# A two-block transformer kernel on one core: router on un-normalised rows, joint square roots, the last three experts written out, and out-projection weights scaled between couples of heads

## What is computed

```
h = rmsnorm(x, g_attn_norm); proj = h @ w_in            # 928 columns
mix = [rmsnorm(pool_mixer(u)), rmsnorm(mla_attention(...))]
x = x + mix @ w_out
h = rmsnorm(x, g_ffn_norm)
x = x + moe(h, w_router, ...)                           # 32 experts, top 4
x = rmsnorm(x, g_final)
# second block, modulated by mod = silu(c) @ w_ada + b_ada
hn = rms(x, norm1_g) * (1 + sc1) + sh1
y = mixer(hn, w_in_2, ...)                              # 16 heads of 3 kinds
x = x + g1 * (y @ w_out_2)
hn = rms(x, norm2_g) * (1 + sc2) + sh2
x = x + g2 * ((silu(gate) * up) @ w_down)               # gate, up = hn @ w_gate_up
```

## Time and profile before

| | |
|---|---|
| median of 3 runs | 1468.03 us (1467.84 to 1472.79) |
| profiled execution: its own time, its span | 1465.46 us, 1463.6 us |
| PE busy | 1409.3 us (96%) |
| PE weight loads | 753.7 us (51%) |
| DVE, ACT, POOL busy | 410.1, 225.0, 21.9 us |
| loaded | 497.05 MB, 340 GB/s on average |
| chain that ended last | PE 74%, DMA 21%, DVE 2%, ACT 1% |

### The profile page before, as it was taken

The page is one execution under the profiler, slowest core; times in us unless marked ns, Lnnn a source line. Parts: engine busy times, 40 slices in busy tenths (PEclk is TensorE's granted clock), DMA queues, the critical chain, the costliest instruction groups (busy, mean ns, idle before and its releaser), DMA issues.

```text
span 1463.6 us, 17945 instructions
## 1 busy us (share of the span) xinstructions
PE 1409.3 (96%) x7194; PEld 753.7 (51%) x7194; DVE 410.1 (28%) x1021; ACT 225.0 (15%) x425; POOL 21.9 (1%) x14
## 2 busy tenths in 40 slices
PE   6998999999999999999999999999899998999999
PEld 5654444444444444344334433443388864888843
DVE  5546311211211111121112111211325563001784
ACT  1332111111111111011101110111123442100000
POOL 3200000000000000000000000000000000000000
PEclk9999999999999999999999999999999999999999
DMA  9978999999999999999999999999994326444400
GB/s 340 354 294 345 413 428 428 428 429 429 428 429 428 429 429 429 428 428 429 429 429 428 428 429 429 429 428 429 415 362 169 115 87 201 141 147 145 160 12 29
DMA packets 83777, 497.05 MB, mean 340 GB/s; under 512 B 6285, under 2 KB 47962, under 8 KB 56762
## 3 DMA queue, kind: packets, MB, share of 16 engines
q1 hardware_dynamic: 83132, 495.46, 83.4%
q10 hardware_dynamic: 606, 1.06, 0.2%
HBM read 495.44 MB, written 1.05 MB: 339 GB/s over the span
## 4 chain that ended last, share of the span: by engine, by line
PE 74%; DMA 21%; DVE 2%; ACT 1%; issue 1%; SPq 0%; DVEq 0%; ACTq 0%
PE PS L955 19%; DMA ring<-in_w_gate_up_dram 13%; PE PS L981 11%; PE PS L1329 11%; DMA qk<-in_w_gate_up_dram 8%; PE PS L940 6%; PE PS L1084 6%; PE PS L1339 5%; PE PS L989 3%; PE PS L773 2%; PE PS L670 2%; PE PS L1208 2%; PE PS L967 1%; PE PS L949 1%; PE PS L962 1%
## 5 line engine op out<-in xcount | busy, mean ns | idle before, releaser
L955 PE MATMUL PS<-ring,store 128*64 128x512 f32 x1360 | 301.0, 594 | 14.0 <-DMA ring<-in_w_gate_up_dram 13.7
L955 PEld LDWEIGHTS PS<-ring,store 128*64 128x64 f32 x1360 | 94.4, 137 | 207.9 <-issue 170.7
L2073 DVE TENSOR_SCALAR store<-PS 128x512 f32<-128x512 f32 x32 | 22.1, 691 | 619.7 <-PE PS L955 619.7
L1329 PE MATMUL PS<-xc,ring 128*128 128x256 f32 x704 | 155.3, 384 | 2.3 <-DVE xc L1769 2.3
L981 PE MATMUL PS<-ring,store 128*64 128x512 f32 x704 | 154.8, 592 | 0.0
L1329 PEld LDWEIGHTS PS<-xc,ring 128*128 128x128 f32 x704 | 135.8, 193 | 21.9 <-DVE xc L1769 2.5
L940 PE MATMUL PS<-store,rows 128*128 128x64 f32 x1056 | 125.2, 272 | 1.3 <-DVE store L2051 1.3
L940 PEld LDWEIGHTS PS<-store,rows 128*128 128x128 f32 x1056 | 123.4, 192 | 2.1 <-issue 2.1
L981 PEld LDWEIGHTS PS<-ring,store 128*64 128x64 f32 x704 | 49.3, 137 | 90.7 <-issue 89.1
L1084 PE MATMUL PS<-ring,xc 128*128 128x240 f32 (+1 forms) x448 | 93.6, 366 | 0.0
L1499 ACT ACTIVATE store<-store 128x512 f32<-128x512 f32 x32 | 20.1, 629 | 452.5 <-DVE store L2073 452.5
(11 more groups left out here) (367 smaller groups left out, 1219.3 us busy)
## 6 DMA issues: line engine op xcount, KB each, us to landing
ring<-in_w_gate_up_dram SPq DMA_DIRECT2D x85, 2048.0 KB, 35.0
ring<-in_w_down_dram SPq DMA_DIRECT2D x44, 2048.0 KB, 37.3
qk<-in_w_gate_up_dram SPq DMA_DIRECT2D x21, 2048.0 KB, 37.5
ring<-in_w_ada_dram SPq DMA_DIRECT2D x24, 1024.0 KB, 15.3
store<-in_w_gate_up_dram SPq DMA_DIRECT2D x11, 2048.0 KB, 34.9
ring<-in_w_gate_up_dram SPq DMA_DIRECT2D x22, 1024.0 KB, 5.1
xc<-in_w_down_dram SPq DMA_DIRECT2D x10, 2048.0 KB, 36.5
store<-in_w_down_dram SPq DMA_DIRECT2D x10, 2048.0 KB, 37.8
```

The costliest lines, as they stand in the source:

```text
L955: mm = pe.matmul(bank(b)[CAP * h:CAP * (h + 1), :], xg[:, k, :], w[:, b * FE + h * 512:b * FE + (h + 1) * 512], start=False, stop=(k == KD ...
L1329: mm = pe.matmul(bank(4 + 2 * (j % 2) + up)[:, f * T:(f + 1) * T], chunk(n)[:, k, f * P:(f + 1) * P], cols[:, k, :], start=(k == 0), stop= ...
```

## The change

The diff touches eight places.

1. **Loads before the experts.** `ada` chunks 8 to 11 (4 MB) move behind the experts; `N_MOE` is four chunks lower. SP's order of the experts' first loads changes, `third[2]` is now at the low end of `store`, and the scratch tiles of the experts are at its high end. The bias of `ada` is loaded once and not 32 times.
2. **Columns one by one.** `need_col(k)` replaces `need_cols`; the products that follow take k in the order 0, 4, 1, 5, 2, 6, 3, 7.
3. **Sums of squares in the mixer.** VectorE adds four columns of squares (`reduce_squares`), and TensorE sums over partitions with 2 products in place of 8, at two places.
4. **Router on un-normalised rows.** x is transposed as each quarter is added; two engines copy without a factor; the gain is multiplied into the router's weights ahead of time; the root is multiplied into the logits. ScalarE copies the parts of the logits and scales the rows.
5. **Order on VectorE** around the choice of rows: ranks are used at once, the gates follow.
6. **Joint roots.** In the two later norms one root serves both tiles; VectorE scales tile 0 and ScalarE tile 1.
7. **Experts.** The last three are written out, and the last one leaves out the gather for a next one. `turn_mod(0, 3)` stands behind expert 0's gate/up.
8. **Second block.** `ada` 14 to 19 stand inside the in-projection, `in2` of chunk 0 goes to bank 3, and `scale_weights` of chunks 1 to 3 stand between couples of heads.

```diff
-ADA_SEGMENTS = (0, 6, 8, 12, 16, 20, 24)
+ADA_SEGMENTS = (0, 6, 8, 16, 18, 20, 24)
-N_MOE = N_OUT1B + 2 + 6
+N_MOE = N_OUT1B + 2 + 2
...
+            for c in (0, 2, 4):
+                load_pair(c)
+            sp.wait_ge(sig["sq_reduced"], 1)
+            load_third(2, 0, 2 * SLOT)
+            sp.wait_ge(sig["scores_done"], HEADS // 2)
+            load_third(0, 0, SLOT)
             sp.wait_ge(sig["scores_done"], HEADS)
+            load_third(0, SLOT, 2 * SLOT)
+            for c in (6, 8):
+                load_pair(c)
             sp.wait_ge(sig["parts_done"], 1)
             load_third(1, SLOT, 2 * SLOT)
+            load_pair(10)
...
+            for t in range(NT):
+                x_ = ffn_order(x_sb[:, t, :])
+                for h in range(2):
+                    pe.wait_ge(sig["x_added"], 2 * t + h + 1)
+                    for k in range(4 * h, 4 * h + 4):
+                        mm = pe.transpose(bank(k // 2)[:, (k % 2) * T + t * P:][:, 0:P], x_[:, k // 2, k % 2, :], ident)
...
-                pe.wait_ge(sig["picked"], nth(e + 2))
-                moe_gather(None, range(KD - 2))
+                if e < EXPERTS - 1:
+                    pe.wait_ge(sig["picked"], nth(e + 2))
+                    moe_gather(None, range(KD - 2))
...
-            with pe.Fori(0, (EXPERTS - 2) // TURN) as i:
+            with pe.Fori(0, (EXPERTS - 2) // TURN - 1) as i:
                 for e in range(2, 2 + TURN):
                     expert(e, i)
+            for e in range(EXPERTS - TURN, EXPERTS):
+                expert(e)
...
             pair_probs(0)
             dve.wait_ge(sig["conv_in"], 2)
             conv_channel(0)
+            keep_ada(4)
             conv_channel(1)
+            keep_mod(2, 3)
...
             conv_silus(0, 1)
+            scale_weights(N_OUT2 + 1)
             pair_probs(2)
             conv_silus(2, 3)
+            scale_weights(N_OUT2 + 2)
             pair_probs(3)
+            scale_weights(N_OUT2 + 3)
             pair_probs(4)
...
-                rsqrt_column(r_[:, at], st[:, at], rsqrt_tmp[:, at])
-                do.tell(v.tensor_scalar(rows[:, t, :], x_sb[:, t, :], r_[:, at], RSQRT_SCALE, ALU.mult, ALU.mult),
-                        "rows_ready")
+            dve.wait_ge(sig["x_squared"], 13)
+            do.step(v.scalar_tensor_tensor(out=mean, in0=st[:, 0:4:2], scalar=EPS, in1=st[:, 1:4:2],
+                                           op0=ALU.add, op1=ALU.add))
+            rsqrt(r_, mean, rsqrt_tmp[:, 0:NT], "rows_ready")
+            do.tell(v.tensor_scalar(rows[:, 0, :], x_sb[:, 0, :], r_[:, 0:1], None, ALU.mult), "rows_ready")
```

More of the change, by code:

```diff
@@ L121, with n_in2 @@
 ADA_AT = [0, 1, N_QB - 2, N_QB - 1, N_KVB + 1, N_KVB + 2, *range(N_OUT1B + 2, N_MOE),
-          *range(N_AFTER, N_IN2), *range(N_OUT2 + 4, N_GU2)]
+          *range(N_AFTER, N_IN2), *(N_IN2 + i for i in (1, 2, 8, 9, 13, 14)), *range(N_OUT2 + 4, N_GU2)]
 ADA_OF = dict(zip(ADA_AT, ADA_CHUNKS))
+def n_in2(c):
+    return N_IN2 + c + 2 * sum(c >= first for first in (1, R_GATES, 9))
+IN2_OF = {n_in2(c): c for c in range(N_CH)}
+assert not set(IN2_OF) & set(ADA_OF)
 def slot_of(n):
@@ L317, in two_blocks @@
[L317 to L324, removed]
@@ new lines, in two_blocks @@
+        g_min, act_buf, sg, act_t, yb = (moe[:, a:a + 512] for a in range(1152, 1152 + 5 * 512, 512))
+        u_clip = moe[:, 3712:4224]
+        sel_b = moe[0:96, 4224:4256].bitcast(BF16)
+        sel_d = moe[0:96, 4256:4288].bitcast(BF16)
+        lg = moe[:, 4288:4360].rearrange("p (t e) -> p t e", t=NT)
+        lr = moe[:, 4360:4432].rearrange("p (t e) -> p t e", t=NT)
+        top = moe[:, 4432:4448].rearrange("p (t e) -> p t e", t=NT)
+        logit_parts = moe[:, 4736:4736 + T]
+        chosen = moe[:, 4448:4512].rearrange("p (t e) -> p t e", t=NT)
@@ L668, in project @@
                     for t in range(NT):
-                        for k in range(KD):
+                        for i, k in enumerate(COLS):
+                            if (c, t) == (0, 0):
+                                need_col(k)
                             mm = pe.matmul(bank(b)[:, t * w:(t + 1) * w], cols[:, k, t * P:(t + 1) * P],
-                                           chunk(n)[:, k, :], start=(k == 0), stop=(k == KD - 1))
+                                           chunk(n)[:, k, :], start=(i == 0), stop=(i == KD - 1))
                     mm.then_inc(chunk_used, 1)
@@ L927, in _ @@
             add_x(4)
+            ada(6)
             pe.wait_ge(sig["routed"], 1)
@@ L1220, in _ @@
                 if c == 0:
+                    ada(14)
+                    ada(15)
+                if c == 1:
                     turn_mod(1, 7)
[L1222 to L1224 removed]
+                if c == 2:
+                    pe.wait_ge(sig["mod_cols"], 2)
                     spread(1, 0, (6, 7))
@@ L1229, in _ @@
             in2(6, 0)
+            ada(16)
+            ada(17)
             pe.wait_ge(sig["heads_cols"], 1)
@@ L2224, in _ @@
                     do.tell(v.tensor_copy(part, bias_bf), "cum_kept")
-            scale_weights(N_OUT2 + 3)
+            dve.wait_ge(sig["bcast_kept"], 1)
+            scale_weights(N_OUT2)
+            keep_ada(3)
             dve.wait_ge(sig["cumt_turned"], 1)
```

401 lines of the change are left out of this document (203 added, 198 removed).

## The result

The changed kernel takes 1455.01 us (median of 4 runs, 1454.64 to 1457.16) beside 1468.76 for the kernel before (4 runs): the ratio is 0.9907, 95% interval 0.9893 to 0.9921. That is 13.75 us less. The forecast was 1448.5, with a range of 1442 to 1459 and a chance of 0.92 for faster: the sign and the range held, but 1455.01 lies outside the forecast's own, narrower range (1444 to 1454), and the gain is a third smaller than the 19.6 of its sum.

A forecast was written before the change was run, and what follows sets the result against it. TensorE's order of work bounds up to 136 us, then loads starting with the first expert, then TensorE again. Terms -11.4 + 0.4 - 1.9 - 3.9 + 3.7 - 6.5 = -19.6 gave 1448.5 us, range 1442 to 1459.

The forecast's parts named there:

- first gate/up at 124 to 126.5: Sign at the start of the experts: the first gate/up product starts there, 136.39 before.
- the end of the last down product 12 to 14 earlier: Sign at the end of the experts: the last down product ends 12 to 14 us earlier than 1048.4.
- Columns one by one: At the start, TensorE goes on after one column on each engine; nearly the whole 1.98 us wait goes: -1.7.
- bringing loads forward is worth nothing by itself: Step on loads before the experts: slots were full, so only an earlier first expert moves the experts' end.
- Square sums: Two places before the experts: four instructions instead of 16, -1.4 at each, less a wait for VectorE; together -1.3.
- Router: Last addition to first gate/up: path shortened by root beside transposes and ranks used at once; -8.4, ends -6 and -9.5.
- `turn_mod` in expert 0: Behind expert 0's gate/up: `turn_mod(0, 3)` delays that expert's later slots, +0.4.
- Last expert: End of the experts: the 2.79 us gather goes, 0.9 of VectorE's product now shows; -1.9, ends 0 and -3.6.
- Norm ahead of the in-projection: Behind the experts: joint root, rows ready for both tiles at 1059.6, chunk 0 ends at 1068.1; -3.9.
- Inside it: Second block's in-projection: moved `ada`, `turn_mod` and `scale_weights`, including a TensorE wait of 1.2; +3.7, ends +2 and +7.
- Last norm: Ahead of the last gate/up: one root starts products earlier, -3.4; the clock holds, -3.1 more; ends -2 and -8.
- the clock fell: Rival: clock falls at a norm (+1 to +3.1) or in the router stretch (+3); time 1452 to 1455, chance 0.20.

The follow-up runs named there:

- before_no_split: The kernel before, with GpSimd's splitting of both biases cut to the first cast of each: 1469.17 us, ratio 1.0009.
- before_collide: The kernel before, with the down bias loaded 10 us earlier and its GpSimd split made to start with the q rotation: 1473.60 us, ratio 1.0032.
- after_again: The changed kernel itself, unaltered, run once more in the last group: 1453.12 us, ratio 0.9896.
- late_down: The changed kernel, with GpSimd's split of the down bias held until the q rotation and the copy of the k rows are done: 1449.96 us, ratio 0.9873.
- two_roots: The kernel with the late split, with a root for each tile again at the last norm and VectorE scaling both tiles: 1454.46 us, ratio 0.9901.
- all_cols: The kernel with the late split, with the first product behind each of three norms waiting for all eight columns again: 1459.61 us, ratio 0.9930.
- both_small: The kernel with the late split, with VectorE's three router memsets earlier and the last three out-projection weight scalings a couple of heads later: 1447.61 us, ratio 0.9852.
- after_no_split: The changed kernel, with GpSimd's splitting of both biases cut to the first cast of each: 1450.82 us, ratio 0.9883.
- ada_first: The kernel of both_small, with VectorE's addition freeing the bank of the out-projection's first products put ahead of the first head's maxima: 1447.33 us, ratio 0.9849.
- split_in_gaps: The kernel of ada_first, with GpSimd's split of the gate/up bias also held until the latent rows are scaled: 1446.19 us, ratio 0.9843.
- root_first: The kernel with the late split, with the router's transposes waiting for VectorE's root and the column copies last: 1457.78 us, ratio 0.9926.

## Why the prediction was right, and where it failed

One number sums up the first stretch: the time from the first in-projection product to the first gate/up.

| | us |
|---|---|
| before, before_no_split, before_collide | 119.4, 119.4, 127.8 |
| forecast (15.3 to 125.0) | 109.7 |
| after, after_again | 117.2, 113.2 |
| late_down, two_roots, all_cols, both_small | 112.4, 111.9, 111.6, 113.6 |
| after_no_split, ada_first, split_in_gaps | 109.9, 108.8, 108.2 |
| root_first | 115.8 |

The prediction was right in sign and range, and the size was off for one main reason, the first stretch. The sign "first gate/up at 124 to 126.5" failed (134.50), and so did "the end of the last down product 12 to 14 earlier" (1045.18 for 1048.4, 3.2 earlier). That the time still lies inside the outer range owes nothing to a term that foresaw the loss.

- **Columns one by one** (-1.7): right as a wait (1.98 became 0.1). In the profile it was eaten by the start: the second chunk of the first `ada` pair landed later, so its products began at 12.41 instead of 11.53, and the turning took 2.92 instead of 1.97. Nine profiles with single columns start L690 at 14.77 to 17.48 (mean 16.1), the four with the wait at 17.00 to 20.28 (mean 18.8). A second worth, half clock avoided, was not in the sum at this place and shows in two of these four only: the products behind the wait take 26.99 in before_collide and all_cols, 25.30 in before and before_no_split.
- **Between this start and 76 us** the prediction had nothing, and here it failed: +7.6 in the out-projection's start (68.84 before, 76.46 after). By rows of TensorE: +0.3 of the start, +1.4 up to L703 (the latent's sums of squares beside GpSimd's split of the gate/up bias), +3.0 up to the turning at L739 (the rotation beside its split of the down bias), +2.9 behind it by half clock. The step that failed is "bringing loads forward is worth nothing by itself": it was argued for the weights alone, and the small loads, which the diff resizes and moves, were priced at nothing with it. GpSimd's second split began 3.6 us earlier (52.7 to 53.0 in three profiles with the change, 56.4 and 57.8 in the two without), and it collided.
- **Square sums** (-1.3): from the out-projection's start to the first addition 41.45 became 40.01, so -1.4.
- **Router** (-8.4): from that addition to gate/up 26.10 became 18.03, so -8.1. root_first shows that at most 5.7 of it is the root's place, some 1.4 of these being half clock that the kernel before did not have.
- **`turn_mod` in expert 0** (+0.4): the second gate/up starts 28.50 behind the first, 27.83 before: +0.7. The loads take it up later: the last gate/up chunk of the last expert starts 1.4 earlier than before, gate/up had started 1.9 earlier.
- **Last expert** (-1.9): from that chunk's start to the last scatter 17.82 became 15.99, so -1.8.
- **Norm ahead of the in-projection** (-3.9): from the last scatter to its first product 16.17 became 13.43, so -2.7. The new bound is the landing of the `ada` chunks behind the experts, until 1056.18; the prediction asked whether the last pair of weights lands, not what lands behind it.
- **Inside it** (+3.7): -5.97 at its first product, -1.96 at the out-projection's (1198.26), so +4.0; the wait of 1.2 was 1.01 and stood where it was said to. Both profiles escaped the half clock that seven others have at the first out-projection products here.
- **Last norm** (-3.4 and -3.1): -3.3 and -2.9. The size held; two_roots and all_cols show that the reason for the clock was half wrong: the idle time right ahead of the products cost it more than the one ahead of the transposes.

The terms behind 136 us gave 6.4 of the 8.2 forecast. The first expert's fell short by 9.5 in the profile: 2.0 at the start, 7.3 in the stretch up to the out-projection, 0.2 behind it. Taking the second split out of the way gives back 3.4 to 5.0 by the ratios (late_down), the other small moves some 4 us more (split_in_gaps, 0.9843). Of the rivals, the clock fell indeed, and the time lies just past the 1452 to 1455 given for it; but it fell at the turning of q and k, behind a collision that no rival named.

The Trainium skill (SBUF — State Buffer, "SBUF: two separate sides") says that VectorE and GpSimd share one pair of ports as an exclusive lock, which a VectorE operation with two inputs in SBUF needs when GpSimd reads SBUF, and that the loser waits for the whole instruction. The rows agree: one multiplication of 128x256 took 0.43 alone and up to 2.23 beside GpSimd's subtraction of 2.2 to 2.4. The kernel before had shown it already, in a place where it cost nothing: one of two equal sums of squares took 4.16 beside a GpSimd operation of 4.12, and 0.43 in before_no_split.

## What to carry to other kernels

Price GpSimd's operations too, and ask of each load that becomes smaller or earlier which engine it starts and what runs there at that moment. An operation that takes several times as long as its equals in the same trace may be held up by a neighbour; look for it before the change meets it. A wait of 2 us right ahead of a long run of products can cost nearly twice its length, or only itself, and a single execution can have the start of such a race on either side: compare stretches between two events over several profiles.

## What the runs showed of the hardware that was not expected

- GpSimd holds up VectorE by whole instructions: four multiplications 6.13 instead of 1.80, one sum of squares of 128 elements 4.03 where 0.29 is its time alone. In after_again a copy of 1024 elements took 2.45 beside GpSimd's subtraction of 2.19, and 0.69 alone, so an operation with one input was held up as well. It goes the other way too: the cast of the down bias took 1.48 next to a copy of 1024 elements on VectorE that started 0.1 earlier, 1.04 in late_down.
- Behind idle times of 2.0 to 2.4 right ahead of products, the next ones ran 1.6 to 1.7 longer at each of three places (all_cols); behind one of 1.98 they ran 1.7 longer in before_collide and not at all in before; behind one of 3.04 with eight transposes between, the transposes took 0.9 longer and the products 0.5 (two_roots); behind 1.34 and 1.01 together, between 0 and 2.9 (5.39 to 8.25 for the same twelve products), and behind 0.70 and 1.58 together nothing in six profiles and 1.2 to 1.7 in seven. What decides from one execution to the next stays open.
